# Chunk inverses on four quarters of the array: upper factor and product moved to the other partition half, lower and upper updates issued in turn

## What is computed

```python
def step(S, inp):
    r_t, w_t, k_t, v_t, kk_t, a_t = inp
    sa = jnp.einsum('bhij,bhj->bhi', S, -kk_t)
    S = (S * w_t[:, :, None, :] + sa[..., None] * (kk_t * a_t)[:, :, None, :]
         + v_t[..., None] * k_t[:, :, None, :])
    return S, jnp.einsum('bhij,bhj->bhi', S, r_t)
```

## Time and profile before

| | |
|---|---|
| median of 3 runs | 4322.28 us (4321.28 to 4325.61) |
| span of the profiled execution | 4323.5 us |
| TensorE busy | 3949.5 us, 91% |
| VectorE busy | 2669.1 us, 62% |
| ScalarE busy | 2122.4 us, 49% |
| GpSimd busy | 1204.6 us, 28% |
| mean granted clock of TensorE | 0.956 |

### The profile page before, as it was taken

One profiled execution on the slowest core, in us unless ns is written; L12 is line 12 of the kernel. 1 busy time (PEld: TensorE's weight loads), 2 busy tenths in 40 slices (PEclk: granted clock), 3 DMA queues, 4 the chain that ended last, 5 costly groups with the idle time before them and its releaser, 6 DMA issues. The chain is left out here.

```text
span 4323.5 us, 76198 instructions
## 1 busy us (share of the span) xinstructions
PE 3949.5 (91%) x31096; PEld 2780.8 (64%) x31096; DVE 2669.1 (62%) x5092; ACT 2122.4 (49%) x3127; POOL 1204.6 (28%) x966
## 2 busy tenths in 40 slices
PE   7989999878988998888789899898999999999889
PEld 5767776546666666666477687686555555555567
DVE  5555555556777787788675323345677777777543
ACT  4444444397777888787443322222333333333431
POOL 1111111125344344434111000000444445454200
PEclk9999999887999999999789999999999999999999
DMA  3334233402111111211255544465232323231243
GB/s 124 95 115 131 83 99 102 124 20 50 34 42 39 47 44 37 56 44 48 86 181 186 197 138 147 167 217 175 52 77 54 80 61 77 55 81 34 99 141 107
DMA packets 388093, 404.95 MB, mean 94 GB/s; under 512 B 115776, under 2 KB 287488, under 8 KB 387488
## 3 DMA queue, kind: packets, MB, share of 16 engines
q1 hardware_dynamic: 386656, 396.77, 31.3%
q10 hardware_dynamic: 1088, 3.32, 0.2%
HBM read 248.36 MB, written 151.62 MB: 93 GB/s over the span
## 5 line engine op out<-in xcount | busy, mean ns | idle before, releaser
L142 ACT ACTIVATE PT<-psum 128x1024 f32<-128x1024 f32 x384 | 394.3, 1027 | 659.6 <-PE psum L132 659.1
L170 DVE TENSOR_REDUCE m<-psum 128x1 f32<-128x1024 f32 x384 | 467.9, 1221 | 274.8 <-PE psum L132 274.8
L132 PE MATMUL psum<-xc,wah 128*128 128x512 f32 x1600 | 514.8, 403 | 3.2 <-DVE xc L146 2.9
L146 POOL TENSOR_TENSOR part<-PT 128x1024 f32<-128x1024 f32 x144 | 341.5, 2371 | 471.4 <-DVE all L146 379.1
L132 PE MATMUL psum<-PT,V 128*64 128x512 f32 x1536 | 371.5, 605 | 0.0
L143 ACT ACTIVATE bias<-score,cand,cols 128x2048 bf16<-128x2048 f32 (+6 forms) x217 | 314.8, 1451 | 85.9 <-DVE cand L153 79.5
L146 POOL TENSOR_TENSOR Lm<-gm,cst 64x512 f32<-64x512 f32 x192 | 257.6, 1342 | 349.9 <-PE psum L132 194.2
L132 PEld LDWEIGHTS psum<-xc,wah 128*128 128x128 f32 x1600 | 300.0, 190 | 79.4 <-issue 10.3
L143 ACT ACTIVATE sgn<-score,cand,cols 128x1920 bf16<-128x1920 f32 (+6 forms) x217 | 291.4, 1343 | 89.5 <-DVE cand L153 84.8
L132 PE MATMUL psum<-hc,w4h 128*128 128x512 f32 x1024 | 320.3, 394 | 8.7 <-DVE w4l L146 8.7
L132 PE MATMUL psum<-xc,wal 128*128 128x512 f32 x800 | 315.9, 395 | 0.0
(11 more groups left out here) (336 smaller groups left out, 8664.9 us busy)
## 6 DMA issues: line engine op xcount, KB each, us to landing
raw_a<-in_w_a SPq DMA_DIRECT2D x50, 512.0 KB
raw_w<-in_w_in SPq DMA_DIRECT2D x32, 512.0 KB, 5.3
QNh<-scr_qnh SPq DMA_DIRECT2D x48, 256.0 KB, 4.9
QRh<-scr_qrh SPq DMA_DIRECT2D x96, 128.0 KB, 4.6
QNl<-scr_qnl SPq DMA_DIRECT2D x48, 256.0 KB, 6.4
xin<-in_x SPq DMA_DIRECT2D x16, 512.0 KB
scr_AR<-AR SPq DMA_DIRECT2D x32, 256.0 KB, 2.2
scr_BK<-BK SPq DMA_DIRECT2D x32, 256.0 KB, 2.2
```

The lines of the kernel that those rows point to most:

```text
L132: return self.e.matmul(out, a, b, start=start, stop=stop, skip_group_check=True)
L142: return self.e.activation(out, src, f, bias=bias, scale=scale)
L146: return self.e.tensor_tensor(out, a, b, op) if self.e else self.vector(out)
L170: return self.e.tensor_reduce(out, a, AX, op, negate=negate) if self.e else self.vector(a)
```

## The change

`Xu`, the product `Y1` and the right-hand side `R` lie, for head `e`, on the other partition half (`o`) than `Xl`, `Lm` and the state `Z` (`a`). So `lv0`, `lvy`, `lvl`, `sa` and `sb` read one half and write the other, while `lvu` and `sm` stay within half `o`. `lvl` and `lvu` of levels 1 to 4 become one piece that issues, for each `n`, two lower and then two upper blocks. Both signals stand behind the last lower and the last upper block. The start value of `Xu` crosses the halves and is made by VectorE in two instructions of 64 partitions; GpSimd no longer makes it, and the waits on it name VectorE.

```diff
                 elif what == "lv0":
                     i = k[1]
-                    q.wait_ge(i_pool, "xu0", i)
+                    q.wait_ge(i_dve, "xu0", i)
...
-                            a = 64 * e
-                            t = q.mm(bank[2][a:a + 64, C * n:C * n + C], Xu[i % 2][a:a + 64, n, :], eye[a:a + 64, :])
+                            a, o = 64 * e, 64 - 64 * e
+                            t = q.mm(bank[2][a:a + 64, C * n:C * n + C], Xu[i % 2][o:o + 64, n, :], eye[o:o + 64, :])
...
-                            t = q.mm(bank[2][a:a + 64, C * n:C * n + C], Lm[lv % 2][a:a + 64, n, :], Xl[a:a + 64, n, :])
+                            a, o = 64 * e, 64 - 64 * e
+                            t = q.mm(bank[2][o:o + 64, C * n:C * n + C], Lm[lv % 2][a:a + 64, n, :], Xl[a:a + 64, n, :])
...
                 elif what == "lvl":
...
-                    for n in range(8):
-                        for e in range(2):
-                            a = 64 * e
-                            t = q.mm(bank[0][a:a + 64, C * n:C * n + C], Xu[i % 2][a:a + 64, n, :], Y1[a:a + 64, n, :])
-                    t.then_inc(*i_pe.up("l", i, lv))
-                elif what == "lvu":
...
                         q.wait_ge(i_dve, "gm", i, 1, 1)
                     for n in range(8):
                         for e in range(2):
-                            a = 64 * e
-                            t = q.mm(bank[1][a:a + 64, C * n:C * n + C], Y1[a:a + 64, n, :], Xu[i % 2][a:a + 64, n, :])
+                            a, o = 64 * e, 64 - 64 * e
+                            l = q.mm(bank[0][a:a + 64, C * n:C * n + C], Xu[i % 2][o:o + 64, n, :], Y1[o:o + 64, n, :])
+                        for e in range(2):
+                            o = 64 - 64 * e
+                            u = q.mm(bank[1][o:o + 64, C * n:C * n + C], Y1[o:o + 64, n, :], Xu[i % 2][o:o + 64, n, :])
+                    l.then_inc(*i_pe.up("l", i, lv))
+                    u.then_inc(*i_pe.up("u", i, lv))
+                elif what == "lvu" and k[2] == 5:
...
-                            t = q.mm(bank[3][a:a + 64, C * h:C * h + C], gm[i % 2][o:o + 64, c, e, h, 0:C], wu[o:o + 64, c, h, e, :],
+                            o = 64 - 64 * e
+                            t = q.mm(bank[3][o:o + 64, C * h:C * h + C], gm[i % 2][o:o + 64, c, e, h, 0:C], wu[o:o + 64, c, h, e, :],
...
-                            t = q.mm(bank[3][a:a + 64, C * h:C * h + C], ar[i % 2][a:a + 64, c, h, 0:C], z[a:a + 64, h, :], False, True)
+                            a, o = 64 * e, 64 - 64 * e
+                            t = q.mm(bank[3][o:o + 64, C * h:C * h + C], ar[i % 2][a:a + 64, c, h, 0:C], z[a:a + 64, h, :], False, True)
...
-                            t = q.mm(bank[3][a:a + 64, 256 + C * h:256 + C * h + C], Xu[i % 2][a:a + 64, 4 * c + h, :], R[a:a + 64, h, :])
+                            a, o = 64 * e, 64 - 64 * e
+                            t = q.mm(bank[3][a:a + 64, 256 + C * h:256 + C * h + C], Xu[i % 2][o:o + 64, 4 * c + h, :], R[o:o + 64, h, :])
...
+                elif what == "lv0":
+
+                    i = k[1]
+                    q.wait_ge(i_pool, "lm", i, 0)
+                    q.wait_ge(s_pe, "b", i - 2, 1)
+                    for e in range(2):
+                        a, o = 64 * e, 64 - 64 * e
+                        t = q.tt(Xu[i % 2][o:o + 64, :, :], Lm[0][a:a + 64, :, :], rep(eye[a:a + 64, :], 8), ALU.add)
+                    t.then_inc(*i_dve.up("xu0", i))
...
-                        q.wait_ge(s_pe, "b", i - 2, 1)
...
-                    if lv == 0:
-                        q.wait_ge(i_pool, "lm", i, 0)
-                        q.tt(Xu[i % 2][:, :, :], m[:, :, :], rep(eye, 8), ALU.add).then_inc(*i_pool.up("xu0", i))
```

More of the change, by code:

```diff
@@ L1317, in pe_2 @@
                         for e in range(2):
-                            a = 64 * e
-                            t = q.mm(bank[1][a:a + 64, C * n:C * n + C], Y1[a:a + 64, n, :], Xu[i % 2][a:a + 64, n, :])
+                            a, o = 64 * e, 64 - 64 * e
[6 more added lines that the diff above has]
+                elif what == "lvu" and k[2] == 5:
+                    i, lv = k[1:]
+                    q.wait_ge(i_act, "y", i, lv)
+                    q.wait_ge(i_dve, "xu", i, lv - 1)
+                    for n in range(8):
+                        for e in range(2):
+                            o = 64 - 64 * e
+                            t = q.mm(bank[1][o:o + 64, C * n:C * n + C], Y1[o:o + 64, n, :], Xu[i % 2][o:o + 64, n, :])
                     t.then_inc(*i_pe.up("u", i, lv))
@@ L1330, in pe_2 @@
                         for e in range(2):
-                            a, o = 64 * e, 64 - 64 * e
-                            t = q.mm(bank[3][a:a + 64, C * h:C * h + C], gm[i % 2][o:o + 64, c, e, h, 0:C], wu[o:o + 64, c, h, e, :],
+                            o = 64 - 64 * e
+                            t = q.mm(bank[3][o:o + 64, C * h:C * h + C], gm[i % 2][o:o + 64, c, e, h, 0:C], wu[o:o + 64, c, h, e, :],
                                      h == 0, False)
```

5 lines of the change are left out of this document (removed).

## The result

The changed kernel takes 4342.54 us, the median of 5 runs (4336.95 to 4346.03), against 4322.28 us before: the ratio is 1.0042, with a 95% interval of 1.0031 to 1.0052. The two medians lie 20.3 us apart; by the ratio it is slower by about 18 us, where 14 us less was forecast, and the time lies outside the range. Its profiled execution spans 4344.2 us at a mean granted clock of 0.947, against 4323.5 us at 0.956.

A forecast was written before the change was run, and what follows sets the result against it. It took the middle stage as a knot of three in-order queues, TensorE tightest; -24 us from TensorE's relief and +10 from VectorE's additions gave -14, so 4322.3 became 4308 us, range 4276 to 4332.

The forecast's parts named there:

- VectorE's term: Start-value additions moved to VectorE in the middle stage: 25% of 39 us arrives at the end, 10 us slower.
- TensorE's term: Lower and upper updates in turn in the middle stage: 40% of 61 us saved arrives at the end, 24 us faster.
- Part 1: Lower and upper updates in turn on four quarters: 15 ns a pass instead of 30, 61 us less over 64 pairs.
- a limit on starts: Rival: long joined bursts held at 22.5 ns a pass, 31 us gained, 12 arriving, less 10; 4320 us, chance 0.05.
- quarters that wait for each other: Rival: quarters of a pair don't overlap over long bursts; 0 gained, 10 lost, 4332 us, chance 0.03.
- Part 2: Signals of the joined updates: lower signal as late as before, uncovered Xl addition costs 0, bounds 0 to +58 us.
- Part 3: Start value Xu moved from GpSimd to VectorE: 32 additions taking 39 us, bounds 22 to 56, and 21 us off GpSimd.
- "Cost 0" for the inverse: Chunk inverse with two VectorE additions for one GpSimd addition: at most 35 us on a lane with slack, cost 0.
- Part 4: Halves swapped in lv0, lvy, sm, sa, sb: cost 0, bounds -5 to +5 us; rewritten order allowed 10 us either way.
- The slower rival: VectorE's additions block the bit search: 56 us, half arriving, while 29% of 61 us arrives; 4332 us, chance 0.17.
- Taken back: Rival: TensorE's relief worth 29%, VectorE's load costs 40% of 39 us; 4320 us, no change, chance 0.22.
- a falling clock: Middle stage: forecast is wrong if the granted clock, 0.94 before, falls because TensorE rests more; no size given.

The follow-up runs named there:

- o_before_work: The kernel before's work (lower burst then upper, start value on GpSimd) issued in the order written for the changed kernel; ratio to before 1.0010.
- m_seq: Changed kernel in its order, GpSimd writing level-0 masks across halves and making the start value, each lower burst issued and signalled before its upper; 1.0005 to before.
- x_mask_same: Changed kernel in its order, updates in turn, but GpSimd writes level-0 masks onto the other half and makes the start value in one instruction; 0.9996 to before.
- x_seq: Changed kernel in its order, start value on VectorE, but each lower burst issued and signalled before its upper burst; 1.0068 to before.
- o_before_dve: o_before_work, but VectorE makes the start value of Xu in two 64-partition instructions within their half; 1.0053 to before.
- d_load: o_before_work plus two 64x512 VectorE additions a unit, with the start value's inputs, whose result nobody reads; 1.0079 to before.
- c_hold: Changed kernel with one added wait: GpSimd starts the level-1 masks only after VectorE's start value; 1.0014 to before.
- x_pool: Changed kernel in its order, but GpSimd makes the start value across the halves in two 64-partition instructions; 1.0024 to before.
- x_mask: x_mask_same with an order the planner writes for it; 0.9996 to before.
- x_double: Changed kernel, plan untouched, each block of the joined lower and upper updates of levels 1 to 4 issued twice; 1.0091 to before.

## Why the prediction was wrong

The parts, each as a step in after's order. They end at the changed kernel by construction; each is a difference of two ratios and known to about 0.14%:

| step | from, to | change |
|---|---|---|
| the new order | before, o_before_work | +0.10% |
| halves swapped | o_before_work, m_seq | -0.05% |
| updates in turn | m_seq, x_mask_same | -0.09% |
| start value on VectorE | x_mask_same, after | +0.46% |
| sum | | +0.42%, 18 us |

*Which steps failed.* Two terms of the sum did, by about as much. VectorE's term was 10 us and came to 20; TensorE's was 24 us and came to 4. With the 2 us by which the order and the halves differ from nothing these are the 32 us between 14 less and 18 more. Taken in the other order (first the start value on VectorE, from m_seq to x_seq, then the updates in turn, from x_seq to the changed kernel) they are 27 and 11 us. Either way both terms missed by 10 to 20 us, and neither alone makes the kernel clearly slower.

*The sum, VectorE's term: mis-sized.* I let 25% of 39 us arrive. 20 us of 35.5 arrived in the changed kernel (56%), 19 of 35.1 in o_before_dve, 30 of 37.3 in d_load. I took the share from waits that VectorE ends in the whole stage and cut it because a bit's wait is mostly the round trip. But the additions sit at one place of VectorE's order, where what stands behind them is soon needed, and the clash lengthens them exactly there: c_hold took 13.6 us off them and 12 us off the end.

*The sum, TensorE's term: mis-sized.* I let 40% of 61 us arrive. Doubling the blocks in the changed kernel takes 21 us (35%) and in x_mask_same 19 us (30%), which looks near; but that also makes the signals 0.9 us later, which the change doesn't. From one after the other to in turn, which is what the change does, 11 us arrive (18%) and 4 us (7%, not told from nothing). In part the relief was smaller than 61 us: TensorE's busy time over the whole program fell by 30 us, and by 43.5 from m_seq to x_mask_same. The granted clock fell too, 0.94 to 0.90 over 836 to 2100, and slower passes fill part of what was saved; how much is not separated.

*Part 1, a pass at 15 ns: right.* 14.5 ns over whole pairs. The four passes of the earlier trace rows alone have three gaps in 0.06 us, 20 ns each; the 15 ns that I read there is right for the 11 passes from 1042.53 to 1042.70 us. The page TensorE: Matmul & The Clock Gate of the Trainium skill ("Wait — 56ns, not 53.3ns?") says that starts are never less than some 25 ns apart; this trace disagrees, and the measurement decides. The rivals that rested on a limit on starts and on quarters that wait for each other fell with it. TensorE's busy time from 836 to 2100 fell by 45.4 us, not by 50 to 60, and part of these is work put off beyond 2100.

*Part 2: the signal is not later, as I said; the bare addition at no cost is not borne out.* VectorE's waits for Xl did not stay at 23.7 us but fell to 8.0; they are 6.3 already in o_before_work, so that is the new order. TensorE's waits for the addition to Xl grew by 5.5 us from m_seq to x_mask_same. What the bare addition costs at the end was not tested by itself; it is within what is missing from TensorE's term.

*Part 3, the additions' duration: right; "Cost 0" for the inverse: not borne out.* Taken 39 us and a mean near 1.2 us, measured 35.5 us and 1.11 us. I held that a start value some 0.1 to 2.2 us later costs the inverse nothing, by the slack of its lane. I also read 14.7 us in 16 waits as a wait for each start value; they are 9 waits, 7 of them listed twice. The pieces behind the start value on TensorE and on GpSimd stand in fixed orders, and TensorE's loads waited 21.6 us for Xu instead of 9.0, GpSimd 20.5. But such waits don't set the price: x_pool has 18.7 us of them at TensorE's loads and 0.28% over x_mask_same, x_mask has 14.3 and no loss, d_load has 7.3 and the largest loss of the three. By which waits the cost reaches the end stays open.

*Part 4: right.* Swapped halves cost nothing (m_seq), the new order 4 us (allowed: 10).

*The rivals.* The slower rival named the right culprit and nearly the right time, but not its path. It was to need a mean above 1.4 us and 20 us more waiting for cand; the mean is 1.11 and the waits grew by 3. So the bit search was not its path. *Taken back* had VectorE's share too small at 40%, and TensorE's too large at 29%.

*The clock.* I named a falling clock as what would make me wrong. It fell (0.74 to 0.59 in the slice 910 to 990), but o_before_work, with long bursts, has 0.61 there, so in this slice the clock falls without shorter bursts too. x_mask_same has 0.57 there and loses nothing, and x_double has 0.92 over the stage, more than the changed kernel, and is slower:

```profile
910.00:990.00 80.00, 45.73 (x656) 34.05 (x655) 32.59 (x100) 75.54 (x82) 19.63 (x19) 0.57 0.14 34
```

```profile
836.00:2120.00 1284.00, 1086.38 (x19837) 777.30 (x19834) 973.86 (x2784) 996.83 (x1487) 514.40 (x424) 0.92 0.17 44
```

No version run here beats the kernel before by more than can be measured. x_mask, with the four quarters and no crossing addition, equals it.

## What to carry to other kernels

Where three in-order engines are knotted together, the share of a microsecond that arrives at the end depends on where in the orders it sits. In this kernel 56 to 80% arrived of what was put on VectorE at one place of each unit, whether its result was needed (the changed kernel) or not (d_load), and 7 to 18% of what shorter bursts were to save on TensorE. A share read from the waits of a whole stage gave neither. A test that doubles an instruction shifts its signals too, and can make a saving look larger than it is. Before moving an operation from GpSimd to VectorE, look at what GpSimd does next to it: if that starts when the moved operation does, count both. If a result must land on other partitions, let the instruction that already writes its input cross over, as x_mask does, instead of adding one.

## What the runs showed of the hardware

- Four 64x64 quarters of the array run side by side over 64 passes of alternating quarters, two of them writing one bank and two the other: 14.5 ns a pass, against some 30 ns on two quarters in the kernel before.
- VectorE's 64x512 addition with both inputs in SBUF takes 0.684 to 1.716 us (mean 1.11) in the changed kernel, where GpSimd's masks run beside it; in c_hold, kept apart from the masks that follow, all 32 lie between 0.678 and 0.689 us. By the page SBUF — State Buffer of the Trainium skill ("Who interferes with whom"), a VectorE instruction with two SBUF inputs contends with a GpSimd instruction that reads SBUF. The trace agrees that they slow each other down: in the stretch shown above the two additions take 3.31 us instead of 1.38, the three masks 4.35 us instead of 3 x 1.27. No run here shows the port. Xu<-Xu,psum, with one input in PSUM, stays at 0.667 to 0.691 us in the same stage.
- With updates in turn, each block issued once, the mean granted clock of 836 to 2120 us was 0.89 to 0.91, with one burst after the other 0.91 to 0.93. The ends of the program didn't follow it: at 0.91 x_mask_same loses nothing, at 0.92 x_double, d_load and o_before_dve lose 0.5 to 0.9%.
